# First expert's slots by comparing and counting, the other experts' rounds between weight splits

## What is computed

```python
aff = softmax((tok @ w_router).astype(f32), axis=-1)   # 512 tokens x 16 experts
cap = 2 * N // 16                                      # 64 tokens for each expert
gate, idx = lax.top_k(aff.T, cap)                      # each expert takes its 64 best tokens
xs = tok[idx]
hid = silu(xs @ w_exp_gate[e]) * (xs @ w_exp_up[e])    # 64 x 2048
out = (hid @ w_exp_down[e]) * gate[..., None]
y = zeros.at[idx].add(out)
```

## Time and profile before

| | us |
|---|---|
| median of 3 runs | 2386.73 |
| the profiled execution, its own time | 2386.68 |
| its span in the trace | 2384.8 |
| PE busy | 2360.4 (99%) |
| DVE busy | 1624.6 (68%) |
| ACT busy | 1488.6 (62%) |
| POOL busy | 401.4 (17%) |

### The profile page before, as it was taken

The page is one execution under the profiler, slowest core; times in us unless marked ns, Lnnn a source line. Parts: engine busy times, 40 slices in busy tenths (PEclk is TensorE's granted clock), DMA queues, the critical chain, the costliest instruction groups (busy, mean ns, idle before and its releaser), DMA issues.

```text
span 2384.8 us, 33778 instructions
## 1 busy us (share of the span) xinstructions
PE 2360.4 (99%) x11804; PEld 1967.3 (82%) x11804; DVE 1624.6 (68%) x1767; ACT 1488.6 (62%) x1707; POOL 401.4 (17%) x279
## 2 busy tenths in 40 slices
PE   8999999999999999999998999999999999999998
PEld 7888888888888888888885888888888888888886
DVE  5545464634546455455346988888888888888897
ACT  5656564533466465554335777777777777777776
POOL 1533433000053324320002000000000000000000
PEclk9999999999999999999999999999999999999999
DMA  6413321125432224112238999999999999999998
GB/s 189 128 45 100 88 73 67 70 98 204 158 98 83 83 62 126 64 63 80 90 155 334 403 393 382 383 383 381 390 387 393 387 383 383 385 387 376 394 375 326
DMA packets 214395, 557.35 MB, mean 234 GB/s; under 512 B 11968, under 2 KB 93376, under 8 KB 209216
## 3 DMA queue, kind: packets, MB, share of 16 engines
q1 hardware_dynamic: 207280, 530.89, 60.4%
q0 software_dynamic: 7056, 25.69, 3.6%
HBM read 533.47 MB, written 23.07 MB: 233 GB/s over the span
## 4 chain that ended last, share of the span: by engine, by line
PE 97%; DVE 1%; DMA 0%; issue 0%; ACT 0%; POOLq 0%; SPq 0%; DVEq 0%; ACTq 0%
PE bank L1433 44%; PE bank L1073 15%; PE bank L1118 13%; PE bank L1039 7%; PE bank L1062 5%; PE bank L1093 3%; PE bank L1236 2%; PE bank L1479 2%; PE bank L1134 2%; PE bank L1217 1%; PE bank L1156 1%; PE bank L1197 1%; PE bank L1203 1%; PE bank L1160 1%; PE bank L1252 0%
## 5 line engine op out<-in xcount | busy, mean ns | idle before, releaser
L2575 DVE TENSOR_TENSOR m_lo<-m_raw,m_hi 128x2048 fp32r<-128x2048 f32 x380 | 867.4, 2290 | 121.0 <-ACT m_hi L1925 117.4
L1925 ACT ACTIVATE m_hi<-m_raw 128x2048 fp32r<-128x2048 f32 x382 | 733.6, 1921 | 261.5 <-PE bank L1433 256.6
L1433 PE MATMUL bank<-m_hi,xs_hi 128*128 128x512 f32 x1032 | 321.0, 392 | 0.0
L1433 PE MATMUL bank<-m_hi,xs_lo 128*128 128x512 f32 x1032 | 317.9, 389 | 0.0
L1433 PE MATMUL bank<-m_lo,xs_hi 128*128 128x512 f32 x1032 | 317.8, 389 | 0.0
L2063 DVE TENSOR_TENSOR w_lo<-w_raw,w_hi 128x1152 fp32r<-128x1152 f32 (+4 forms) x110 | 145.0, 1344 | 180.1 <-ACT w_hi L1561 180.0
L1433 PEld LDWEIGHTS bank<-m_lo,xs_hi 128*128 128x128 f32 x1032 | 193.7, 188 | 40.5
L1433 PEld LDWEIGHTS bank<-m_hi,xs_lo 128*128 128x128 f32 x1032 | 193.7, 188 | 40.4
L1433 PEld LDWEIGHTS bank<-m_hi,xs_hi 128*128 128x128 f32 x1032 | 191.4, 188 | 38.2 <-DVE xs_lo L2597 0.2
L1073 PE MATMUL bank<-h_hi,w_hi 128*128 128x512 f32 x512 | 203.0, 396 | 0.0
L1073 PE MATMUL bank<-h_lo,w_hi 128*128 128x512 f32 x512 | 199.6, 390 | 0.0
(11 more groups left out here) (292 smaller groups left out, 4239.4 us busy)
## 6 DMA issues: line engine op xcount, KB each, us to landing
m_raw<-in_w_exp_gate SPq DMA_DIRECT2D x128, 1024.0 KB, 8.1
m_raw<-in_w_exp_up SPq DMA_DIRECT2D x128, 1024.0 KB, 7.6
m_raw<-in_w_exp_down SPq DMA_DIRECT2D x128, 1024.0 KB, 7.4
w_raw<-in_w_b SPq DMA_DIRECT2D x66, 512.0 KB, 6.2
w_raw<-in_w_a SPq DMA_DIRECT2D x24, 1024.0 KB, 5.1
w_raw<-in_w_c SPq DMA_DIRECT2D x24, 1024.0 KB, 4.8
w_raw<-in_w_d SPq DMA_DIRECT2D x8, 1024.0 KB, 6.5
xt<-in_x SPq DMA_DIRECT2D x8, 512.0 KB, 7.9
```

The source lines that it names most:

```text
L1433: mm = pe.matmul(ps[:, half, :], a[:, chunk + k, :], v[:, k, 512 * half:512 * (half + 1)], start=first and k == n == 0, stop=last and k == ...
L1925: act.activation(m_hi[slot.slot][:, :, :], m_raw[raw.slot][:, :, :], ACT.Copy)\
L2575: dve.tensor_tensor(m_lo[slot.slot][:, :, :], m_raw[raw.slot][:, :, :], m_hi[slot.slot][:, :, :].bitcast(F32), ALU.subtract)\
```

## The change

The first expert's 128 slots are found another way. For each group (the letters below, `of` is the group) PE lays the group's 512 affinities for expert 0 on all partitions of a PSUM bank ("t": a transpose of a broadcast column for each tile). DVE compares them with each token's own affinity, tile against tile ("r", 5 steps: 4 for ties and 4 for greater, on 512, 384, 256 and 128 columns), with the row sums taken along. PE counts the other half of the comparisons ("c", 6 small matmuls). DVE takes one from the other, which gives each token's rank, and marks its slot ("o"). PE multiplies the marks with (token, affinity) pairs ("q", 4 matmuls), and DVE writes the first column of `m_index` and `m_gate` and `index_get` ("p"). Group 0's t, r, c and o are done in the projection stage of the seam, and its q at the end. The constants come with `ret_tables`' tensor and are loaded to `rank_table` by SP.

The eight rounds for the experts 1 to 15 are the same instructions as before, but DVE runs them after the first gather is issued, between the lo splits of the first expert; the merge, the transposes of the lists and the writing of the other 15 columns follow inside the first expert, and the second gather waits for these. The splits of the units 1, 4, 7 and 13 are POOL's, after the first gather and ahead of the second. The filler matmuls between the rounds are gone, those after them are 4 and not 6, and one is added ahead of "c" of group 1. The first expert is taken out of the loop.

```diff
-WARM_START, WARM_FIRST, WARM_GATHER, WARM_SPLIT, WARM_NORM = 3, 1, 6, 2, 4
-WARM_ROUNDS = {1: 1, 2: 1, 3: 1, 4: 1, 5: 1, 6: 1, 7: 1}
+WARM_START, WARM_FIRST, WARM_GATHER, WARM_SPLIT, WARM_NORM = 3, 1, 4, 2, 4
-EARLY_SPLITS = 2
+POOLED = (1, 4, 7, 13)
@@ closing_schedule
+        if last and i == NT - 2:
+            out += [("t", 0, i) for i in range(NT)]
+    if last:
+        out += [("r", 0, j) for j in range(NT + 1)]
+    out += [("D", 1, 0), *((("c", 0), ("o", 0)) if last else ()), ("Y", 0), ...
...
-                ("N", 3), ("k", 2), ("e", 0), ("l", 2), ("L", 3), ("E", 1), ("k", 3), ("e", 1), ("l", 3),
-                ("E", 2), ("E", 3), ("e", 2), ("b", 0), ("e", 3), ("B", 3)]
+                ("N", 3), ("k", 2), ("e", 0), ("l", 2), ("L", 3), ("t", 1, 0), ("E", 1), ("k", 3), ("e", 1), ("l", 3),
+                ("t", 1, 1), ("E", 2), ("E", 3), ("e", 2), ("t", 1, 2), ("e", 3), ("t", 1, 3), ("q", 0), ("b", 0),
+                ("Z", 1), ("r", 1, 0), ("r", 1, 1), ("r", 1, 2), ("r", 1, 3), ("r", 1, 4), ("c", 1), ("o", 1), ("q", 1), ("p", 1),
+                ("B", 3)]
@@ gpsimd
-            for i in range(EARLY_SPLITS):
-                pool.wait_ge(s_mhi, i + 1)
-                pool.tensor_tensor(m_lo[i][:, :, :], m_raw[i][:, :, :], m_hi[i][:, :, :].bitcast(F32),
-                                   ALU.subtract).then_inc(s_mlo, 1)
             all_stored(pool, NB)
...
             pool.tensor_copy(index_add[:, 0:1], m_index[:, 0:1]).then_inc(s_asked, 1)
+            for k in POOLED:
+                raw, cut = k % RAW_SLOTS, k % SPLIT_SLOTS
+                pool.wait_ge(s_mhi, k + 1)
+                pool.tensor_tensor(m_lo[cut][:, :, :], m_raw[raw][:, :, :], m_hi[cut][:, :, :].bitcast(F32),
+                                   ALU.subtract).then_inc(s_plo, 1)
+            pool.wait_ge(s_route, 2)
             pool.wait_ge(s_mtr, 2)
             pool.wait_ge(s_gather, 16)
             gather(1, 1)
@@ tensor
+                elif what == "t":
...
+                    pe.wait_ge(s_aff, of * NT + i + 1)
+                    pe.transpose(ranked[of][:, natural(i)], aff[:, i, 0:1].to_broadcast([P, P]), ident[:, :])\
+                        .then_inc(s_rows, 1)
+                elif what == "c":
...
+                    for j in range(NT - 1, 0, -1):
+                        pe.wait_ge(s_beats, i * NT + NT - j)
+                        for k in range(j):
+                            last = pe.matmul(counts[i], beats[j][:, natural(k)], unit_cols[:, k, :],
+                                             start=j == NT - 1 and k == 0, stop=j == 1)
+                    last.then_inc(s_counts, 1)
+                elif what == "q":
+                    pe.wait_ge(s_hot, i + 1)
+                    for k in range(NT):
+                        last = pe.matmul(pick[CAP * i:CAP * (i + 1), :], hot[:, i, k, :], value[:, i, k, :],
+                                         start=k == 0, stop=k == NT - 1)
+                    last.then_inc(s_picked, 1)
...
-            for k, times in enumerate(WARM_ROUNDS.values()):
-                pe.wait_ge(s_round, k + 1)
-                keep_busy(times, ps_proj[:, 0, :])
...
+            def lists_turned():
+                pe.wait_ge(s_best, 1)
+                for k, a in enumerate((chosen_at, chosen)):
+                    pe.transpose(ps_d[0:CAP, k, 0:48], a[0:48, :], ident[0:48, 0:48]).then_inc(s_listed, 1)
+            def up_cols(lists=False):
...
+                    if lists and j == 0:
+                        lists_turned()
@@ vector
+            def compared(of, nth):
+                if nth < NT:
...
+                    dve.scalar_tensor_tensor(tie[j][:, 0:cols], ranked[of][:, 0:cols], aff[:, j, 0:1],
+                                             later[:, T - cols:], ALU.is_equal, ALU.mult).then_inc(s_link, 1)
...
+                if nth > 0:
...
+                    dve.scalar_tensor_tensor(beats[j][:, :], ranked[of][:, 0:cols], aff[:, j, 0:1], tie[j][:, 0:cols],
+                                             ALU.is_gt, ALU.add, accum_out=row_sum[:, of, j:j + 1]).then_inc(s_beats, 1)
...
+                elif what == "o":
...
+                    then(dve.tensor_tensor(row_sum[:, i, 0:NT - 1], row_sum[:, i, 0:NT - 1], counts[i], ALU.subtract))
+                    dve.tensor_tensor(hot[:, i, :, :], slots, row_sum[:, i, :].unsqueeze(2).to_broadcast([P, NT, CAP]),
+                                      ALU.is_equal).then_inc(s_hot, 1)
+                elif what == "p":
+                    dve.wait_ge(s_picked, NB)
+                    dve.tensor_copy(index_get[:, 0:1], pick[:, 0:1]).then_inc(s_first, 1)
...
+            eight_best(0)
             dve.wait_ge(s_asked, 1)
-            dve.wait_ge(s_mlo, EARLY_SPLITS)
...
             split_units(1)
+            split_unless_pooled()
+            eight_best(1)
             transposed_lo(xs_hi, xs_lo)
-            split_units(SPLIT_SLOTS - EARLY_SPLITS - 1)
+            split_units(2)
+            after()
+            split_unless_pooled()
+            eight_best(2)
+            split_units(1)
+            eight_best(3)
+            split_units(1)
+            split_unless_pooled()
+            eight_best(4)
+            eight_best(5)
+            after()
+            split_units(3)
+            hidden_step()
+            split_units(1)
+            eight_best(6)
+            after()
+            split_units(1)
+            split_unless_pooled()
+            eight_best(7)
+            halves_merged()
+            transposed_lo(hid_hi, hid_lo)
+            split_units(1)
+            routes()
+            split_units(1)
...
```

More of the change, by code:

```diff
@@ L414, in hybrid_encoder @@
         assert cursor[0] <= att_at
+        cursor[0] = ret_at
+        rank_table, _, _ = put("rank_table", [P, RANK_COLS], F32)
+        slots = rank_table[:, 0:NT * CAP].rearrange("p (i s) -> p i s", i=NT)
+        later = rank_table[:, NT * CAP:NT * CAP + T]
+        value = rank_table[:, NT * CAP + T:].rearrange("p (b i k) -> p b i k", b=NB, i=NT)
+        tie = [put(f"tie{i}", [P, T], BF16)[0] for i in range(NT)]
+        beats = [put(f"beats{j}", [P, P * (j + 1)], BF16)[0] for j in range(NT)]
+        hot, _, _ = put("hot", [P, NB, NT, CAP], F32)
+        row_sum, _, _ = put("row_sum", [P, NB, NT], F32)
+        unit_cols, _, _ = put("unit_cols", [P, NT - 1, NT - 1], BF16)
+        assert cursor[0] <= att_at
         cursor[0] = att_at
@@ L440, in hybrid_encoder @@
         part_sums = [a[:, k, P:2 * P] for a in (ps_sc, ps_out) for k in range(2)]
+        ranked = [ps_out[:, 1, :], ps_proj[:, 1, :]]
+        counts = [ps_sc[:, 0, 256 + 4 * b:256 + 4 * b + NT - 1] for b in range(NB)]
+        pick = ps_sc[:, 1, 256:258]
         ps_g, ps_t, ps_u, ps_d = bank
@@ L602, in tile_read, with lo_ready @@
             eng.wait_ge(s_proj_free[proj.slot], START + proj.lap + 1)
+        def lo_ready(eng, unit, behind=0):
+            k = unit.k - behind
+            if k in POOLED:
+                eng.wait_ge(s_plo, POOLED.index(k) + 1)
+            else:
+                eng.wait_ge(s_mlo, unit.n(1 - behind - sum(each < k for each in POOLED)))
         def all_stored(eng, count):
@@ L1502, in down, with expert @@
                     use(ps_d, hi, lo, MK * j, f == 0 and j == 0, f == 1 and j == 3)
-            def expert(e, last):
+            def expert(e, last, lists=False, shift=0):
+                e2, e16 = e * 2 + 2 * shift, e * 16 + 16 * shift
                 gate_cols()
-                hidden_transposes(e * 2 + 1)
-                up_cols()
+                hidden_transposes(e2 + 1)
+                up_cols(lists)
                 if last:
@@ L1534, in _ @@
             up_cols()
-            with rolled(pe, NE - 1, mt, {"unit": 24, "slot": 24, "tr": 6, "step": 2}) as e:
-                expert(e, False)
+            expert(0, False, True)
+            with rolled(pe, NE - 2, mt, {"unit": 24, "slot": 24, "tr": 6, "step": 2}) as e:
+                expert(e, False, shift=1)
             expert(NE - 1, True)
@@ L2532, in _, with eight_best @@
             all_read(dve, s_tr_free, tr)
-            for r in range(CAP // 8):
+            def eight_best(r):
                 eight = slice(8 * r, 8 * r + 8)
@@ L2677, in last_expert, with split_unless_pooled @@
                                          ALU.mult, ALU.mult).then_inc(s_rowout, 1)
+            def split_unless_pooled():
+                if unit.k in POOLED:
+                    for x in (raw, slot, unit):
+                        x.k += 1
+                else:
+                    split_units(1)
+            eight_best(0)
             dve.wait_ge(s_asked, 1)
-            dve.wait_ge(s_mlo, EARLY_SPLITS)
-            for x in (raw, slot, unit):
-                x.k += EARLY_SPLITS
             split_units(1)
+            split_unless_pooled()
+            eight_best(1)
             transposed_lo(xs_hi, xs_lo)
-            split_units(SPLIT_SLOTS - EARLY_SPLITS - 1)
+            split_units(2)
```

(13 more changed lines are left out.)

120 lines of the change are left out of this document (79 added, 41 removed).

## The result

| | before | after |
|---|---|---|
| median, us | 2387.25 (6 runs, 2386.29 to 2388.41) | 2398.68 (6 runs, 2396.68 to 2399.86) |
| profiled execution, its own time | 2386.68 | 2399.86 |
| its span | 2384.8 | 2398.1 |
| mean granted clock of PE | 0.997 | 0.993 |

The ratio of the medians is 1.0048 [1.0036, 1.0059]: the change makes the kernel slower by 11.4 us. The forecast was 2394, with a range to 2402. The profiled execution of after is the slowest of its six, 1.2 us above their median.

What follows compares the result with a forecast made beforehand. PE bounds the kernel, its chain holding 97% of the span, with DVE nearly full in the experts. Terms -3.4 + 2.4 + 2.0 + 1.0 + 5.2 = +7.2 us on 2386.7 gave 2394; own range 2388 to 2401, 8-in-10 range 2383.5 to 2402.

Steps and rivals of the forecast that it cites:

- The start, 3.4 us earlier: Seam before the first expert: earlier list and first gather bring the first useful expert matmul 3.4 us forward (bounds 0.3, 6.6).
- PE's added work: Projection stage: group 0's four transposes and 6 count matmuls delay all that follows by 1.2 us (0.9 to 1.7).
- T: Moment of the first expert's first useful matmul: 1286.74 us before the change, forecast at 1283.3.
- Units 6 and 7, 2.4 us: First expert: the shared port makes PE wait 3.7 us if POOL is first, 1.1 if DVE is; middle taken, 2.4.
- Units 12 and 13, 2.0 us: First expert, same port conflict: PE waits 2.6 us if POOL is first, 0.8 if not; 2.0 taken.
- The rival by which only the data matter: First expert: the port does not matter, splits at units 6, 7, 12, 13 cost nothing; +0.6, 2387.3 us, chance 0.25.
- Units 14 and 15, 1.0 us: First expert: their splits now follow the hidden tile's rest, so PE waits 1.0 us (bounds 0.7, 1.3).
- The second gather, 5.2 us: Inside the first expert: it waits for the list copies, lands 10.3 us after them, PE waits 5.2 (bounds 0.9, 6.7).
- a rival of 0.15: PE's clock falls in the new waits: 2.5 us for each of two falls; +12.2, 2399 us, chance 0.15.
- locks and late gather: The forecast's main case: port lockouts between POOL's and DVE's splits plus the late second gather; +7.2 us, 2394, chance 0.50.

Runs made afterwards that it cites:

- with six fillers: The changed kernel with seven filler matmuls, not four, before the first `xs` and six more before the second `xs`'s transposes: 2394.96 us, 1.0039 of before.
- the filler runs: The changed kernel with seven fillers before first `xs` (2396.09 us); plus eleven (2396.18) or six (2394.96) before second `xs`; six plus three before unit 12 (2395.94).
- without its two faults: The changed kernel with only unit 1 split by POOL and the second gather using the first expert's list, without its wait: 2386.89 us, 1.0004 of before.
- with the rounds in the shadow: The changed kernel with rounds 0 to 6 run during the store and first gather, POOL splitting units 0 and 1, seven fillers: 2385.16 us, 0.9992 of before.
- with the loads held back too: The kernel with rounds in the shadow, loads from unit 4 on held until the first gather's issue, later rounds between units: 2382.99 us, 0.9982 of before.

## Why the prediction was near, and what in it failed

The direction and the mechanism held, the time was 4.7 us low. Its steps:

- *The start, 3.4 us earlier.* It was 3.34, out of parts that were not right, so the match is in part luck. PE's added work was put at 1.2 us; the projection ended 0.3 us later than before (1256.26 against 1255.98). The list came at 1270.15 (1271.0 was said), so the store's landing at 1270.85 still ended the wait, and POOL issued at 1271.91, not 1272.9. The gather took 8.05 us, 7.5 was said, within the bounds. DVE's first split and round 1, which the forecast had last before T (1282.5), were done at 1281.00. What ended last was PE at half clock: 3.4 us from the landing to T, where 2.35 stood before.
- *Units 6 and 7, 2.4 us.* It was 0.7. DVE had the port first and POOL's unit 7 was late, by less than the 1.1 of that case.
- *Units 12 and 13, 2.0 us.* It was 2.6. POOL was first, and this is the price given for that case. The page "SBUF — State Buffer" of the Trainium skill, section "SBUF: two separate sides", calls the shared port an exclusive lock for the whole instruction, whoever starts first; the four pairs above agree, 6.54, 3.74 and 6.12 us on one side and 6.68 on the other. The rival by which only the data matter fell with them.
- *Units 14 and 15, 1.0 us.* There was no wait. PE's slow unit 12 is not the reason: with six fillers unit 12 went at full clock and PE did not wait either (unit 14 was split at 1326.87 and wanted at 1327.37). By then PE was 3.3 us late by the waits at the units 7 and 12, which this term left out.
- *The second gather, 5.2 us.* PE waited 5.8. It landed 12.8 us after the list copies (1327.81 to 1340.63), where 10.3 was said and 11.8 was the upper bound: the issue took 2.23 us as said, but the transfer met a queue that was nearly full, since SP's loads ran on while PE stood: the DMA share was 0.66 in 1331 to 1333 us, 0.89 to 1336 and 1.02 from there to the landing. PE came 2.0 us later to it than reckoned (7.1 after the list copies, not 5.1), which hid most of that.
- *The step that failed is the clock's place.* It stood as a rival of 0.15 ("Against it: each wait alone is short"), at 2.5 us for each of two falls, and outside the sum. It fell three times, for 5.2 us in all, and once after 2.61 us of standing. The mechanisms did not exclude one another: locks and late gather make the waits, and the waits the falls.

What the miss is made of can be read in the trace of after. The forecast's terms put the second `xs` at T+55.6 (45 + 2.4 + 2.0 + 1.0 + 5.2); it came at T+57.3, 1.7 later, since the gather landed 2.5 us later after the list copies than said. The half clock behind it cost 2.8 more, for which the sum had nothing. 7.2 + 1.7 + 2.8 = 11.7, the difference by the end of unit 23; 11.4 was measured by the medians. The whole 5.2 must not be added to the sum: 1.8 of them, in unit 12, were not on the path. That the falls cost time in the medians is not shown: the filler runs moved these by 1.1 to 2.6 us, within their spread. In the traces it is 1.8 us for the first fall and 2.5 for the one at the second gather.

The gain of the change itself had also been rightly sized at little: without its two faults it came out at 1.0004, and with the rounds in the shadow at 0.9992. Only with the loads held back too was there a gain to be measured, 4.0 us for a start 6.4 us earlier. How much of an earlier start arrives depends on the execution too: the first transpose of `xs` lies between 1279.4 and 1281.5 us in after and the seven experiments that are alike up to there but for fillers, the later experts run at one of two paces, and there is one profile for each.

## What to carry to other kernels

When a chain on one engine is shortened, the work taken off it has to be put where that engine's consumers wait for something else, not just behind the next issue: here the kernel with the rounds between the splits took 2398.7 us, and the one with seven of the eight in the 10 us in which a store and a gather were under way 2385.2. A second engine for elementwise work is no second engine if both share a port: three of the four splits given to GpSimd were worth nothing. Price a wait of TensorE together with the half clock behind it, but only where it is on the path that ends last: here PE stood for 2.6 us at unit 12 and then ran slowly, and the second gather came no later for it.

## What the runs showed that I had not expected

- One indirect gather of 512 KB took 4.9 to 5.1 us behind an emptying or held-back load queue and 7.8 to 11.7 us beside full-rate loads. A plain store of 512 KB, a few us earlier, gained nothing by holding back the loads of unit 4 and later: 10.9 us. PE waited for no unit because of the loads held back.
- PE's granted clock went to half after it stood for 2.6 us in five profiled executions, and stayed at full after the same 2.6 us in a sixth.
- In steady state one expert takes 67.96 us in some profiled executions (before and eight experiments) and 68.06 in others (after, the one with both causes removed, the fastest kernel), 1.5 us over fifteen experts, with the same instructions. The cause stays open.
